# Attention's output projection as three fp32r products of rounded parts and rests, in a one-core transformer kernel on Trainium2

## The reference, cut to what matters

```
mix = concat([rmsnorm(y_pool, g_out_pool), rmsnorm(y_attn, g_out_attn)], axis=-1)
x = x + mix @ w_out            # mix is 256 x 1024, w_out 1024 x 1024
h = rmsnorm(x, g_ffn_norm)
x = x + moe(h, w_router, ...)  # 32 experts, top 4; 12.6 MB of fp32 weights each
return rmsnorm(x, g_final)
```

## Time and profile before

| what | us |
|---|---|
| three runs | 1499.5, 1500.98, 1501.61 (median 1500.98) |
| the profiled execution's own time | 1502.64 |
| its span, first to last instruction | 1500.8 |
| expert jobs begin (first gate-up matmul) | 549.58 |
| TensorE busy | 1424.4 |
| DVE, POOL, ACT busy | 648.0, 407.2, 245.3 |

### The profile page before, as it was taken

The page is one execution under the profiler, slowest core; times in us unless marked ns, Lnnn a source line. Parts: engine busy times, 40 slices in busy tenths (PEclk is TensorE's granted clock), DMA queues, the critical chain, the costliest instruction groups (busy, mean ns, idle before and its releaser), DMA issues.

```text
span 1500.8 us, 20320 instructions
## 1 busy us (share of the span) xinstructions
PE 1424.4 (95%) x7328; PEld 781.7 (52%) x7329; DVE 648.0 (43%) x1094; ACT 245.3 (16%) x422; POOL 407.2 (27%) x430
## 2 busy tenths in 40 slices
PE   8999999999989999999899999999899999999995
PEld 7768876999976664334334343343334333333332
DVE  2034744766754444333443344343434434333233
ACT  1122113444422320001001010010000000100001
POOL 3000001322216014343533434443543444200000
PEclk9999999999999999999999999999999999999998
DMA  7343334555443948999996999999999999999995
GB/s 259 128 140 141 112 113 145 181 179 196 152 153 134 353 176 351 429 428 428 427 428 277 430 428 427 427 428 428 428 427 428 428 428 427 428 429 429 427 427 212
DMA packets 77413, 480.73 MB, mean 320 GB/s; under 512 B 7019, under 2 KB 31272, under 8 KB 52808
## 3 DMA queue, kind: packets, MB, share of 16 engines
q1 hardware_dynamic: 74046, 477.45, 78.2%
q10 hardware_dynamic: 3338, 2.88, 0.6%
HBM read 479.26 MB, written 1.05 MB: 320 GB/s over the span
## 4 chain that ended last, share of the span: by engine, by line
PE 49%; DMA 40%; POOL 4%; DVE 3%; issue 2%; ACT 1%; POOLq 1%; SPq 0%; DVEq 0%; ACTq 0%
DMA stage<-in_w_gate_up 30%; PE bank L2072 9%; PE bank L1592 9%; PE bank L1826 8%; DMA ring<-in_w_gate_up 7%; PE bank L1602 7%; PE bank L2148 5%; PE bank L1838 4%; POOL ring L593 4%; PE bank L1758 2%; DMA ring_b<-in_w_gate_up 2%; DMA ring_b<-in_w_down 2%; PE bank L2053 1%; PE bank L2107 1%; POOLq L586 0%
## 5 line engine op out<-in xcount | busy, mean ns | idle before, releaser
L593 POOL COPY ring<-stage 128x1024 f32<-128x1024 f32 x300 | 309.4, 1077 | 446.2 <-DMA stage<-in_w_gate_up 360.5
L2072 PE MATMUL bank<-ring,x_T 128*64 128x512 f32 x1584 | 369.8, 613 | 37.6 <-POOL ring L593 30.1
L2072 PEld LDWEIGHTS bank<-ring,x_T 128*64 128x64 f32 x1584 | 111.4, 140 | 273.4 <-issue 206.4
L2148 PE MATMUL bank<-ring_b,act_T 128*64 128x512 f32 x1056 | 237.5, 600 | 1.0 <-ACT act_T L860 0.5
L1472 DVE TENSOR_TENSOR h<-h,bank 128x512 f32<-128x512 f32 x128 | 82.2, 684 | 244.3 <-PE bank L2107 244.3
L2148 PEld LDWEIGHTS bank<-ring_b,act_T 128*64 128x64 f32 x1056 | 72.5, 137 | 148.8 <-issue 127.9
L2072 PE MATMUL bank<-ring_b,x_T 128*64 128x512 f32 x528 | 120.6, 598 | 2.3 <-DMA ring_b<-in_w_gate_up 2.3
L1592 PE MATMUL bank<-x_nT,ring 128*128 128x256 f32 x512 | 114.9, 387 | 2.6 <-issue 2.6
L1448 DVE SCALAR_TENSOR_TENSOR y_lo<-bank,slot_gate,y_hi 128x512 fp32r<-128x512 f32 x33 | 24.8, 751 | 196.6 <-ACT y_hi L840 196.6
L1592 PEld LDWEIGHTS bank<-x_nT,ring 128*128 128x128 f32 x512 | 98.9, 194 | 17.3 <-issue 3.5
L854 ACT ACTIVATE sig<-bias_raw 128x512 f32<-128x512 f32 x33 | 20.8, 629 | 509.2 <-DVE bias_raw L1478 509.2
(11 more groups left out here) (426 smaller groups left out, 1562.8 us busy)
## 6 DMA issues: line engine op xcount, KB each, us to landing
stage<-in_w_gate_up SPq DMA_DIRECT2D x75, 2048.0 KB, 25.0
ring_b<-in_w_down SPq DMA_DIRECT2D x64, 2048.0 KB, 22.9
ring_b<-in_w_gate_up SPq DMA_DIRECT2D x32, 2048.0 KB, 21.0
ring<-in_w_gate_up SPq DMA_DIRECT2D x21, 2048.0 KB, 25.5
ring<-in_w_in SPq DMA_DIRECT2D x22, 1024.0 KB, 7.3
ring<-in_w_ffn_in SPq DMA_DIRECT2D x22, 1024.0 KB, 5.1
ring<-in_w_ffn_out SPq DMA_DIRECT2D x11, 1024.0 KB, 4.9
ring<-in_w_out SPq DMA_DIRECT2D x8, 1024.0 KB, 6.2
```

The lines of the kernel that those rows point to most:

```text
L593: ins = pool.tensor_copy(pair_slot(g, pair)[:, cols], t.stage[:, pair, cols])
L2072: ins = pe.matmul(banks[n][rows, :], t.x_T[:, c, :], job_slot(g, c)[:, c0:c0 + 512], start=False, stop=(c == GU - 1), skip_group_check=True)
L2148: ins = pe.matmul(banks[4][rows, :], t.act_T[:, k, SLOTS * (c // 2):SLOTS * (c // 2) + SLOTS], job_slot(g, GU + c)[:, c0:c0 + 512], start= ...
```

## The change

Attention's four `pa` banks are made of fp32r products instead of fp32 ones. ACT rounds both weight chunks to `pa_hi` between the exponentials and the `pt` drains; POOL writes the rests over the chunks in the ring (`ring_r` is the ring's memory under an fp32r type), ahead of `rsqrt("mla")`; DVE writes `ya_hi` where it wrote `ya_T`, and then, in eight instructions of 128 x 128, the rests `ya_lo`, ahead of the mean squares. Each bank takes twelve fp32r matmuls in place of four fp32 ones; the last four wait for `ya_lo`. `pa_hi` lies in the memory of the first down slots, `ya_lo` in that of the second staged pair, so `load_down(0, 0)`, `load_stage(1, 1)` and `load_stage(1, 2)` move behind `pa11`, behind `load_gu(0, 2)`. `ring` also becomes the first persistent buffer, ahead of `x_n` and `h`.

```diff
@@ SP
     load_gu(0, 3)
-    for h in range(2):
-        load_down(0, h)
+    load_down(0, 1)
     sp.wait_ge(*g.r2.filled("pp11"))
     load_gu(0, 1)
     sp.wait_ge(*g.r2.filled("av1"))
     load_stage(1, 0)
-    sp.wait_ge(*g.r2.filled("yt1"))
     sp.wait_ge(s.msq_ready, NORM_AT["mla"] + 1)
+    sp.wait_ge(*g.r2.filled("pa11"))
+    load_gu(0, 2)
+    load_down(0, 0)
     for pair in range(1, AHEAD):
         load_stage(1, pair)
-    sp.wait_ge(*g.r2.filled("pa11"))
-    load_gu(0, 2)
@@ POOL
     rsqrt("pool")
+    for c in range(2):
+        slot = slot_use(g.n_second + 9 + c)[0]
+        pool.wait_ge(s.pa_rounded, c + 1)
+        pool.tensor_tensor(t.ring_r[:, slot, :], t.ring[:, slot, :], t.pa_hi[:, c, :].bitcast(F32),
+                           ALU.subtract).then_inc(s.pa_split, 1)
     rsqrt("mla")
@@ ACT
     for h in range(MH):
         soft(h)
+    act.wait_ge(s.diff_ready, 1)
+    act.wait_ge(s.q_roped, 1)
+    for c in range(2):
+        slot, value = slot_use(g.n_second + 9 + c)
+        act.wait_ge(s.landed[slot], value)
+        act.activation(t.pa_hi[:, c, :], t.ring[:, slot, :], ACT.Copy).then_inc(s.pa_rounded, 1)
@@ DVE
-        dve.tensor_tensor(t.ya_T[:, :, b * P:(b + 1) * P], bank[:].rearrange("p (k n) -> p k n", k=4),
-                          spread(vec(t, "g_out_attn", 0, 4), P), ALU.mult).then_inc(done, 1)
+        dve.tensor_tensor(t.ya_hi[:, :, b * P:(b + 1) * P], bank[:].rearrange("p (k n) -> p k n", k=4),
+                          spread(vec(t, "g_out_attn", 0, 4), P), ALU.mult).then_inc(s.ya_rounded, 1)
+    for b in range(NB):
+        bank, done = out_of(r2, f"yt{b}")
+        toks = slice(b * P, (b + 1) * P)
+        dve.wait_ge(s.ya_rounded, b + 1)
+        for k in range(4):
+            ins = dve.scalar_tensor_tensor(out=t.ya_lo[:, k, toks], in0=bank[:, k * P:(k + 1) * P],
+                                           scalar=vec(t, "g_out_attn", k), in1=t.ya_hi[:, k, toks].bitcast(F32),
+                                           op0=ALU.mult, op1=ALU.subtract)
+        ins.then_inc(done, 1)
@@ TensorE
-    pe.wait_ge(*r2.drained("yt1"))
+    def attended_out(c, b):
+
+        bank, slot = open_bank(r2, f"pa{c}{b}"), slot_use(n + 9 + c)[0]
+        pe.wait_ge(s.pa_rounded, c + 1)
+        pe.wait_ge(s.pa_split, c + 1)
+        pe.wait_ge(s.ya_rounded, b + 1)
+        y_hi, y_lo = ([m[:, k, b * P:(b + 1) * P] for k in range(4)] for m in (t.ya_hi, t.ya_lo))
+        w_hi, w_lo = ([m[:, 512 * k:512 * k + 512] for k in range(4)] for m in (t.pa_hi[:, c, :], t.ring_r[:, slot, :]))
+        for k in range(4):
+            pe.matmul(bank[:], y_hi[k], w_hi[k], start=(k == 0), stop=False)
+            pe.matmul(bank[:], y_hi[k], w_lo[k], start=False, stop=False)
+        pe.wait_ge(*r2.drained(f"yt{b}"))
+        for k in range(4):
+            ins = pe.matmul(bank[:], y_lo[k], w_hi[k], start=False, stop=(k == 3))
+        ins.then_inc(s.filled2, 1)
+
     for c, b in ((0, 0), (0, 1), (1, 0), (1, 1)):
-        project_out("pa", t.ya_T, c, b)
+        attended_out(c, b)
@@ memory
+        self.ring_r = new("ring_r", [RING, CW], F32R)      # freed again before "ring" is placed
...
-        self.ya_T = new("ya_T", [4, T])
+        self.ya_hi = new("ya_hi", [4, T], F32R)
...
+    def last_out(self, new):
+
+        new("under_rope_q", [4096])
+        self.pa_hi = new("pa_hi", [2, CW], F32R)
+        new("under_y_sq", [12736])
+        self.ya_lo = new("ya_lo", [4, T], F32R)
```

More of the change, by code:

```diff
@@ L232, in build @@
         t = Buffers()
+        with ExitStack() as stack:
+            t.rounded(into(stack))
         t.persistent(into(ctx))
-        for phase in (t.mixer, t.ffn, t.attention, t.experts):
+        for phase in (t.mixer, t.ffn, t.attention, t.last_out, t.experts):
             with ExitStack() as stack:
@@ L2271, in __init__ @@
         self.y_ready = new("y_ready")
+        self.ya_rounded = new("ya_rounded")
+        self.pa_rounded = new("pa_rounded")
+        self.pa_split = new("pa_split")
         self.ff_zero = new("ff_zero")
@@ L2363, with rounded @@
 class Buffers:
+    def rounded(self, new):
+        self.ring_r = new("ring_r", [RING, CW], F32R)
     def persistent(self, new):
+        self.ring = new("ring", [RING, CW])
+        self.x_n = new("x_n", [NB, D])
         self.h = new("h", [NB, D])
-        self.x_n = new("x_n", [NB, D])
-        self.ring = new("ring", [RING, CW])
         self.ident = new("ident", [P])
```

## The result

The kernel after ran in 1498.43 us (median of 13, 1496.44 to 1500.24), the kernel before beside it in 1502.23 (median of 13, 1499.2 to 1505.0). The ratio is 0.9977, with a 95% interval of 0.9969 to 0.9984: 3.5 us faster, 2.4 to 4.7. In a later series of twelve more runs the unchanged kernel after came to 0.9972 (0.9961 to 0.9982). The forecast was 3.5 us. One more execution, of the experiment with the loads behind `jobs_ready`, took 1806.84 us at a mean granted clock of 0.84 of full and is left out of every ratio.

What follows compares the result with a forecast made beforehand. The prediction took the expert stage as transfer-bound, but its end as set by TensorE's path from 512 to 549 us. 0.8 + 2.86 - 0.2 = 3.5 us takes the median from 1500.98 to 1497.5, range 1494.8 to 1501.0.

Steps and rivals of the forecast that it cites:

- What bounds the kernel: TensorE's path from 512 to 549 us: whatever it gets shorter by, the end gets earlier by, despite a transfer-bound expert stage.
- The start, 0.8 us: Before `pa00`: PE waits only for the first block of `ya_hi`, not both, and starts at 519.3; gain 0.8 us.
- The products, 2.86 us: Attention's output projection: 48 fp32r matmuls at 0.228 us take 10.96 us instead of 13.82; gain 2.86 us.
- DVE's rests, 0.2 us: Eight DVE instructions for `ya_lo`, 0.31 us each: PE rests 0.2 us before the third products of `pa00`.
- What they push back: Mean squares, root and adds behind DVE's rests come later; hidden, with 0.3 us to spare before PE wants `pa01`.
- ACT and POOL: ACT's two copies at 1.90 us leave 4.2 us of cover; POOL's two subtractions at 4.63 cost nothing, cover 7 us.
- The moved loads: Four 2 MB transfers behind `pa11` land by 553.7 us, in the stream's gap from 542 to 561; cost nothing, 4.0 us left.
- The 1.2 GHz clock through part of this stretch: Slower rival: clock at 1.2 GHz through the projection, all 48 products cost 10.9 us more, time 1508.4; chance 0.06.
- DVE's eight would cost 0.485 us each: Part of the part-gain rival (0.24): DVE's rests at 0.485 us each cost 1.2 us in all, time 1498.5.
- products at 3/4: Rival: fp32r products start every 0.216 us in the projection and take 10.4 us, time 1496.9; chance 0.05.
- the stream did not swallow the gain: Rival judged here: the end hangs on the transferred bytes alone, time 1501.0; chance 0.06.
- its nearest rival, 1498.5 for a part of the gain given back: Part of the gain is given back: by DVE's eight, 1498.5, or by another clock fall, 1499.2; chance 0.24 together.

Runs made afterwards that it cites:

- The loads alone: Kernel before with the moved loads and new memory order, but its fp32 products and no rounding: 1501.53 us, ratio 1.0001 to the kernel before.
- the experiment with two products: Kernel after without the sixteen matmuls of `ya_lo` by the rounded weights; DVE still writes the rests: 1496.77 us, ratio 0.9967 to the kernel before.
- in the experiment POOL waited: Kernel after with the four 2 MB loads behind the filling of bank `rk` instead of `pa11`: 1497.28 us, ratio 0.9972 to the kernel before.
- the kernel with filled rests: Kernel after with dummy matmuls ahead of `av0` and of the first gate-up pair, where TensorE rests: 1498.33 us, ratio 0.9975 to the kernel before.

## Why the prediction was right, point by point

- **What bounds the kernel.** Right. What TensorE's path gains reaches the end, as far as the runs can tell: 3.38 us in the trace between the transposes and the router, 3.5 (2.4 to 4.7) in the ratio. The loads alone change nothing within 1.5 us. The gaps of the stream moved and did not close.
- **The start, 0.8 us.** Right: the first product starts 518.08 - 517.40 = 0.68 us after the start of the last transposes. Before, those started at 518.65, 0.66 us long, and the first product at 520.09, 1.44 us after. The gain is 0.76; undone, it costs 0.85.
- **The products, 2.86 us.** Slightly too high. 36 products take 526.51 - 518.08 = 8.43 us, 0.234 each, and the last twelve 530.17 - 527.30 = 2.87; that is 11.30 us where I had 10.96. The pace is 0.232 instead of the feed-forward's 0.228, and each of the two starts behind transposes costs another 0.1. Against it the transposes between take 0.79 for 0.88. The net is 2.62. The estimate from the four-pass count of the Trainium skill (FP8 and Floating Point Precision, "TensorE Precision Notes"), three quarters of a fp32 product's time, was 10.4 us; the trace, with 11.30, is further from it than my row was.
- **DVE's rests, 0.2 us.** Too high, it is nothing: TensorE starts the third products at 520.02 us, with no rest, and the first four of DVE's, 0.26 us apart and 0.34 long, end at 518.70 + 3 x 0.26 + 0.34 = 519.8. I took 0.31 us for each; start to start they take 0.26, the straight line between the two neighbours without my addition. The rows were right, the allowance on them was not needed.
- **What they push back.** Right that it is hidden; the spare time was 1.0 us and not 0.3. In the experiment with two products I then put DVE's part too low, at 1 us where it took back 1.9.
- **ACT and POOL.** Right: 3.69 and 9.02 us, at the places named, with 4.45 and 7.7 us left.
- **The moved loads.** Right, and with more cover than I counted. I gave 4.0 us until POOL wants the staged pair; in the experiment POOL waited 3.9 us in all for staged pairs without a loss in the time, since it came out of POOL's next rest, and the gap near 590 us took what was left for the stream.
- **The rivals.** The 1.2 GHz clock through part of this stretch does occur, at a cost of 5.7 us in one profiled execution. It was one of the two with fp32 products; none of the eight with fp32r products has it, so nothing ties it to the change. That DVE's eight would cost 0.485 us each did not come (0.26), nor did products at 3/4, and the stream did not swallow the gain.
- **The time.** 1497.5 was given for a median of 1500.98; with the median of before at 1502.23 beside it the same 3.5 us give 1498.7, and 1498.43 was measured. Some luck is in how close that is. The gain on the products was put 0.24 us too high and DVE's cost 0.2 us too high, and the two errors cancel: 0.76 + 2.62 is 3.38 for the 3.46 of the sum. And the time alone would not have told the account from its nearest rival, 1498.5 for a part of the gain given back; the trace does.

## What to carry to other kernels

A transfer-bound stretch does not make work ahead of it free: look for the gaps in the stream, for where it starts and stops by an engine's leave, that engine's path sets the end. The same gaps tell how late a load may come, and an experiment that takes the cover away (four loads behind the first use, 9 us) shows where the limit is more surely than the times of first use do. When fp32 products are split in three (the product of the two rests is left out, here as in the feed-forward network), price them at the pace of the same products in the same kernel, 0.232 us for 512 columns here against 0.864 for a whole fp32 product, and look at once at the engine that makes the rests: here it was the next to bind.

## What the runs showed of the hardware that was not expected

- The granted clock fell to half for 13 us, from 514 to 527, in one of ten profiled executions (before, after and the experiments); in the other nine it was at 1.00 from 505 to 530. TensorE was busy all through the windows on both sides of the fall. Its last rest had been one of 0.97 us, until 511.06, and eight of the nine others have the same rest at the same place. Shorter stretches below full clock stand at other places: between 430 and 440 us in six of the ten (0.59 from 432 to 436 us in the kernel after run again), and not in the other four.
- The first gate-up pair, behind a rest of 0.41 us in all but the kernel with filled rests, took 3.65 us in six executions and 5.16 to 5.35 in four, and of the kernel after itself 5.16 in one and 3.65 in the other. A difference of 1.7 us between two profiles is no evidence of an edit.
- The clock of the first 60 us was 0.94, 0.97 or 1.00 in different executions, with 1.2 us between the first two. The runs of one kernel scatter over 4 to 8 us, and the time goes with the mean granted clock: in the two series, the runs of the kernel before at 0.990 of full took 1498.9 us on average (3 runs), those at 0.984 took 1504.8 (3 runs). The clock does not explain all of it, as the kernel after took from 1496.4 to 1500.2 us at one and the same 0.988. It took a dozen runs a side to tell 3.5 us from this scatter.
